# Feed-forward gated activations turned by VectorE block transposes instead of TensorE

## Reference

```python
D_FF = -(-8 * D_MODEL // (3 * 256)) * 256      # 5632

def swiglu(h, w_gate, w_up, w_down):
    return (jax.nn.silu(h @ w_gate) * (h @ w_up)) @ w_down

# in second_block, for each of 2 layers, after the mixer:
x = x + swiglu(rms_norm_2(x, norm_ffn[i]), ffn_w_gate[i], ffn_w_up[i], ffn_w_down[i])
```

## Time and profile before

| what | value |
|---|---|
| time, median of 3 runs | 3035.3 us |
| lowest and highest run | 3033.88 and 3035.71 us |
| span of the profiled execution | 3032.1 us (no other time of this execution is given) |
| TensorE busy | 3024.7 us |
| VectorE busy | 1712.5 us |
| ScalarE busy | 1546.5 us |
| GpSimd busy | 299.9 us |
| first FfnUp stage | about 1239 to 1728 us of the span |
| first FfnDown stage | about 1728 to 1965 us of the span |

### The profile page before, as it was taken

The page is one execution under the profiler, slowest core; times in us unless marked ns, Lnnn a source line. Parts: engine busy times, 40 slices in busy tenths (PEclk is TensorE's granted clock), DMA queues, the critical chain, the costliest instruction groups (busy, mean ns, idle before and its releaser), DMA issues.

```text
span 3032.1 us, 37463 instructions
## 1 busy us (share of the span) xinstructions
PE 3024.7 (100%) x14305; PEld 2532.1 (84%) x14305; DVE 1712.5 (56%) x2011; ACT 1546.5 (51%) x2125; POOL 299.9 (10%) x252
## 2 busy tenths in 40 slices
PE   9999999999999999999999999999999999999999
PEld 8888888988888888888888888888888888888887
DVE  5666655589555675544444455568855444444554
ACT  5556554555654664544444444467845444444443
POOL 1043200145000450000000000001000000000000
PEclk9999999999999999999999999999999999999999
DMA  9674335555445544555655555565455556555554
GB/s 312 199 234 154 129 128 180 164 184 175 139 157 190 181 152 140 185 190 181 197 189 180 195 193 193 190 201 178 140 200 188 183 185 199 184 183 196 192 192 151
DMA packets 256721, 551.84 MB, mean 182 GB/s; under 512 B 9728, under 2 KB 43264, under 8 KB 245856
## 3 DMA queue, kind: packets, MB, share of 16 engines
q1 hardware_dynamic: 255824, 548.79, 54.5%
q0 software_dynamic: 752, 1.48, 0.2%
q10 hardware_dynamic: 32, 0.01, 0.0%
HBM read 548.14 MB, written 2.10 MB: 181 GB/s over the span
## 4 chain that ended last, share of the span: by engine, by line
PE 98%; DVE 1%; ACT 0%; DMA 0%; issue 0%; SPq 0%
PE psum L734 42%; PE psum L2364 32%; PE psum L2502 16%; PE psum L2640 2%; PE psum L1462 2%; PE psum L1478 1%; PE psum L976 1%; PE psum L1490 1%; PE psum L2333 1%; PE psum L1451 1%; PE psum L2091 0%; DVE weights_lo L550 0%; PE psum L1686 0%; PE psum L1962 0%; PE psum L1465 0%; DMA proj<-in_mem 0%
## 5 line engine op out<-in xcount | busy, mean ns | idle before, releaser
L550 DVE TENSOR_TENSOR weights_lo<-weights,weights_hi 128x1024 fp32r<-128x1024 f32 (+2 forms) x1015 | 1259.1, 1251 | 1018.0 <-ACT weights_hi L532 1016.4
L532 ACT ACTIVATE weights_hi<-weights 128x1024 fp32r<-128x1024 f32 (+2 forms) x1015 | 1052.1, 1047 | 1200.2 <-PE psum L734 549.4
L734 PE MATMUL psum<-weights_hi,act_hi 128*128 128x512 f32 (+3 forms) x1952 | 764.3, 392 | 0.3 <-DVE weights_lo L550 0.2
L734 PE MATMUL psum<-weights_hi,act_lo 128*128 128x512 f32 (+3 forms) x1952 | 749.1, 384 | 0.0
L734 PE MATMUL psum<-weights_lo,act_hi 128*128 128x512 f32 (+3 forms) x1952 | 748.1, 383 | 0.0
L2364 PE MATMUL psum<-weights_hi,act_hi 128*128 128x512 f32 x1408 | 549.8, 391 | 0.0
L2364 PE MATMUL psum<-weights_hi,act_lo 128*128 128x512 f32 x1408 | 548.1, 389 | 0.0
L2364 PE MATMUL psum<-weights_lo,act_hi 128*128 128x512 f32 x1408 | 547.8, 389 | 0.0
L734 PEld LDWEIGHTS psum<-weights_hi,act_hi 128*128 128x128 f32 x1952 | 366.7, 188 | 69.1 <-issue 4.6
L734 PEld LDWEIGHTS psum<-weights_hi,act_lo 128*128 128x128 f32 x1952 | 366.3, 188 | 68.0
L734 PEld LDWEIGHTS psum<-weights_lo,act_hi 128*128 128x128 f32 x1952 | 367.2, 188 | 62.9
(11 more groups left out here) (262 smaller groups left out, 1921.3 us busy)
## 6 DMA issues: line engine op xcount, KB each, us to landing
weights<-in_ffn_w_gate SPq DMA_DIRECT2D x88, 1024.0 KB, 5.1
weights<-in_ffn_w_up SPq DMA_DIRECT2D x88, 1024.0 KB, 5.1
weights<-in_ffn_w_down SPq DMA_DIRECT2D x88, 1024.0 KB, 4.8
weights<-in_odd_w_in SPq DMA_DIRECT2D x40, 1024.0 KB, 5.1
weights<-in_even_w_in SPq DMA_DIRECT2D x36, 1024.0 KB, 5.0
weights<-in_w_out SPq DMA_DIRECT2D x32, 1024.0 KB, 5.0
weights<-in_rnn_w_in SPq DMA_DIRECT2D x32, 1024.0 KB, 5.3
weights<-in_attn_w_qkv SPq DMA_DIRECT2D x24, 1024.0 KB, 5.2
```

Source lines behind the costliest of these rows:

```text
L532: e.nc.scalar.activation(e.WH[(2 * slot + b) % HL][:, 0:n // 2], e.RAW[slot][:, b * n // 2:(b + 1) * n // 2], ACT.Copy).then_inc(self.hi.s ...
L550: e.nc.vector.tensor_tensor(e.WL[s][:, 0:n // 2], e.RAW[slot][:, b * n // 2:(b + 1) * n // 2], e.WH[s][:, 0:n // 2].bitcast(F32), ALU.subt ...
L734: last = e.nc.tensor.matmul(e.PS[:, banks.start + m, 0:w], a, x, start=(kk == 0 and n == 0), stop=(kk == KT - 1 and n == 2))
```

## The change

The turn of a chunk moves from TensorE to VectorE. A VectorE transpose turns 32x32 blocks; one instruction takes the 32 partitions (tokens) of block row `rows` of `HID`, and of every 128 channels the 32 of block column `cols`, for both row tiles and all four channel tiles: 2 x 4 x 32 = 256 elements a partition. It writes them turned to the 32 partitions of block column `cols` of `HT`. Sixteen such instructions turn one chunk, from SBUF to SBUF.

In FfnUp they are issued in pairs behind each of the eight low halves of granules 2 to 5 of the next chunk. For the last chunk they are issued in the first group of FfnDown: three behind each of the four low halves of granules 1 and 2, two behind each of the two of granule 3. The TensorE turn, ScalarE's copy and the waits on `hcopied` are gone. TensorE waits at the second half of the first down granule for the product alone (`hid`). ScalarE waits in groups 0 and 10 of FfnDown for the turned chunks. VectorE's FfnUp program is written out for all 11 chunks in place of a loop; TensorE's loop starts one chunk earlier.

```diff
@@ -275,6 +275,7 @@
         e.s_pv = Signal(ctx, nc, "s_pv")
         e.s_stored = Signal(ctx, nc, "s_stored")
         e.s_gate = Signal(ctx, nc, "s_gate")
+        e.s_blockturned = Signal(ctx, nc, "s_blockturned")
         e.s_hid = Signal(ctx, nc, "s_hid")
         e.s_hturned = Signal(ctx, nc, "s_hturned")
         e.s_hcopied = Signal(ctx, nc, "s_hcopied")
@@ -2221,14 +2222,16 @@
 
 class FfnUp(Stage):
 
+    BLOCKS = 16
+
     def __init__(self, e, prev, prep):
         gm = e.queue.pop(0)
         self.n = D_FF // CHUNK
         self.flip = e.parity
         self.views = gm["gate"]["view"], gm["up"]["view"]
         super().__init__(e, prev, 8 * self.n, prep)
-        self.gate, self.hid, self.hturned, self.hcopied = (s.mark() for s in (e.s_gate, e.s_hid, e.s_hturned, e.s_hcopied))
-        for s in (e.s_gate, e.s_hid, e.s_hturned, e.s_hcopied):
+        self.gate, self.hid, self.hturned = (s.mark() for s in (e.s_gate, e.s_hid, e.s_blockturned))
+        for s in (e.s_gate, e.s_hid, e.s_blockturned):
             s.advance(self.n)
         prep.end()
 
@@ -2248,16 +2251,6 @@
 
         return 2 * ((part + self.flip) % 2)
 
-    def copy_hidden(self, act, f):
-
-        e = self.e
-        act.wait_ge(self.hturned.sem, self.hturned.at(f + 1))
-        e.nc.scalar.activation(e.HT[:, bass.ds(f * 4, 4), :].rearrange("p k t -> p (k t)"),
-                               e.PS[:, 4:6, :].rearrange("p b n -> p (b n)"), ACT.Copy).then_inc(self.hcopied.sem, 1)
-
-    def carry_scalar(self, act):
-        self.copy_hidden(act, self.n - 1)
-
     def scalar(self, act):
         e = self.e
 
@@ -2269,8 +2262,6 @@
                     if q == 1:
                         self.prev.carry_scalar(act)
                     self.prep.after_hi(act, q)
-            if not first:
-                self.copy_hidden(act, f - 1)
             for q in range(4):
                 self.split_hi(act, f * 8 + 4 + q, q, f * 2 + 2)
                 if q == 0:
@@ -2292,55 +2283,53 @@
         e = self.e
         dve.wait_ge(self.used.sem, self.used.at(f * 16 + 16))
         dve.wait_ge(self.gate.sem, self.gate.at(f + 1))
-        if not isinstance(f, int) or f > 0:
+        if f > 0:
 
             dve.wait_ge(self.hturned.sem, self.hturned.at(f))
         for m in range(MT):
             ins = e.nc.vector.scalar_tensor_tensor(e.HID[:, m, :], e.PS[:, self.bank(1) + m, :], e.RS[:, m:m + 1], e.GATE[:, m, :], ALU.mult, ALU.mult)
         ins.then_inc(self.hid.sem, 1)
 
+    def turn(self, dve, f, first, count):
+
+        e = self.e
+        if first == 0:
+            dve.wait_ge(self.hid.sem, self.hid.at(f + 1))
+        for n in range(first, first + count):
+            rows, cols = divmod(n, 4)
+            src = e.HID[32 * rows:32 * rows + 32, :, :].rearrange("p m (k x c) -> p m k x c", k=4, x=4)[:, :, :, cols, :]
+            dst = e.HT[32 * cols:32 * cols + 32, 4 * f:4 * f + 4, :].rearrange("p k (m x t) -> p m k x t", m=MT, x=4)[:, :, :, rows, :]
+            ins = e.nc.vector.transpose(dst, src)
+        if first + count == self.BLOCKS:
+            ins.then_inc(self.hturned.sem, 1)
+
     def carry_vector(self, dve):
         self.product(dve, self.n - 1)
 
+    def carry_turn(self, dve, first, count):
+        self.turn(dve, self.n - 1, first, count)
+
     def vector(self, dve):
-        for q in range(4):
-            self.split_lo(dve, q, q)
-            if q == 1:
-                self.prev.carry_vector(dve)
-            self.prep.after_lo(dve, q)
-        for q in range(4):
-            self.split_lo(dve, 4 + q, q)
-
-        def body(f):
-            for q in range(4):
-                self.split_lo(dve, f * 8 + q, q)
-                if q == 1:
-                    self.product(dve, f - 1)
-            for q in range(4):
-                self.split_lo(dve, f * 8 + 4 + q, q)
-        body(1)
-        with dve.Fori(2, self.n) as f:
-            body(f)
-
-    def turn(self, pe, f, first):
-
-        e = self.e
-        pe.wait_ge(self.hid.sem, self.hid.at(f + 1))
-        if not first:
-            pe.wait_ge(self.hcopied.sem, self.hcopied.at(f))
-        for k in range(4):
-            for m in range(MT):
-                last = e.nc.tensor.transpose(e.PS[:, 4 + k // 2, (k % 2) * T + m * P:(k % 2) * T + (m + 1) * P],
-                                             e.HID[:, m, k * P:(k + 1) * P], e.CT[:, 0:P])
-        last.then_inc(self.hturned.sem, 1)
-
-    def carry_tensor(self, pe):
-        self.turn(pe, self.n - 1, False)
+        for f in range(self.n):
+            for g in range(8):
+                slot = 2 * (g - 2)
+                turning = f > 0 and 0 <= slot < self.BLOCKS // 2
+                between = (lambda dve, j: self.turn(dve, f - 1, 2 * slot, 2)) if turning else None
+                self.split_lo(dve, f * 8 + g, g % 4, between=between)
+                if turning:
+                    self.turn(dve, f - 1, 2 * slot + 2, 2)
+                if g == 1:
+                    if f == 0:
+                        self.prev.carry_vector(dve)
+                    else:
+                        self.product(dve, f - 1)
+                if f == 0 and g < 4:
+                    self.prep.after_lo(dve, g)
 
     def tensor(self, pe):
         e, prep = self.e, self.prep
 
-        def products(f, part, turn_at=None):
+        def products(f, part):
             first = isinstance(f, int) and f == 0
             for q in range(4):
                 if first and part == 0:
@@ -2366,14 +2355,10 @@
                     last.then_inc(self.used.sem, 1)
                 if first and part == 0:
                     prep.after_tensor(pe, q)
-                if q == 2 and turn_at is not None:
-                    self.turn(pe, *turn_at)
         products(0, 0)
         products(0, 1)
-        products(1, 0, (0, True))
-        products(1, 1)
-        with pe.Fori(2, self.n) as f:
-            products(f, 0, (f - 1, False))
+        with pe.Fori(1, self.n) as f:
+            products(f, 0)
             products(f, 1)
 
 
@@ -2440,15 +2425,18 @@
     def scalar(self, act):
         final = self.n - 1
 
+        up = self.prev
+
         def body(j):
+            if isinstance(j, int):
+
+                act.wait_ge(up.hturned.sem, up.hturned.at(up.n - 1 if j == 0 else up.n))
             for q in range(4):
                 if not (isinstance(j, int) and j == final and q == 3):
                     self.hidden_hi(act, j, q)
                 if isinstance(j, int) and j == final and q == 2:
                     self.hidden_hi(act, j, 3)
                 self.split_hi(act, j * 4 + q, q, j + 1)
-                if isinstance(j, int) and j == 0 and q == 1:
-                    self.prev.carry_scalar(act)
         body(0)
         with act.Fori(1, final) as j:
             body(j)
@@ -2464,9 +2452,13 @@
                     self.hidden_lo(dve, j, q)
                 if isinstance(j, int) and j == final and q == 2:
                     self.hidden_lo(dve, j, 3)
-                self.split_lo(dve, j * 4 + q, q)
-                if isinstance(j, int) and j == 0 and q == 0:
+                carry = isinstance(j, int) and j == 0
+                at = (None, (0, 3), (6, 3), (12, 2))[q]
+                self.split_lo(dve, j * 4 + q, q, between=(lambda dve, j: self.prev.carry_turn(dve, *at)) if carry and q else None)
+                if carry and q == 0:
                     self.prev.carry_vector(dve)
+                elif carry:
+                    self.prev.carry_turn(dve, at[0] + at[1], at[1])
         body(0)
         with dve.Fori(1, final) as j:
             body(j)
@@ -2516,9 +2508,7 @@
                         if first and h == 0 and m == 0:
                             pe.wait_ge(up.gate.sem, up.gate.at(up.n))
                         if first and h == 1 and m == 0:
-                            up.carry_tensor(pe)
-                        if first and h == 1 and m == 1:
-                            pe.wait_ge(up.hcopied.sem, up.hcopied.at(up.n))
+                            pe.wait_ge(up.hid.sem, up.hid.at(up.n))
                         last = self.products(None, h, m, hh, hl, q, (2 * q + h) % HL, 0, first)
                     last.then_inc(self.used.sem, 1)
                     if q == 1 and isinstance(j, int) and j == final:
```

## The result

The changed kernel takes 3014.54 us, median of 5 runs (3014.22 to 3019.92), against 3035.53 us before in the same comparison (5 runs, 3033.88 to 3040.33). The ratio of its runs to those of before is 0.9936, with a 95% interval of 0.9925 to 0.9947: 19.4 us less, between 16 and 23 (the two medians lie 21.0 apart). The profiled span is 3012.7 us. The prediction was 3015.9 us, with a span of 3012.7. It was right.

What follows compares the result with a forecast made beforehand. The prediction took TensorE's queue to bound the kernel. Removing the turns (19.1 us) and the wait for the copy (0.3), with added VectorE work costing 0, gave 19.4 off 3035.3: 3015.9 us, range 3012 to 3024.

Steps and rivals of the forecast that it cites:

- The turn: TensorE's transposes of each chunk leave its queue: 22 turns at 0.87 us, 19.1 us gained.
- The copy's wait: TensorE's idle time in two places until ScalarE's copy had emptied the banks goes away: 0.3 us gained.
- From span to time: Median of the runs stays 3.2 us above the profiled span, so span 3012.7 means time 3015.9 us.
- The transpose, t = 0.43: Start-to-start price of one VectorE block transpose, taken from subtraction L2438 on as many elements: 0.43 us.
- The covers: VectorE's idle time hides transposes up to 1.14 us each in the up stage, 0.68 in the down stage; cost 0.
- 16t - 18.3: Up stage: lateness of low half 12 in us per chunk with t us per transpose; positive only above 1.14.
- VectorE's new waits and the written-out program: VectorE's up stage: waiting for the previous chunk's turned signal, and writing out the loop, cost 0.
- the tightest point of the chunk: Up stage: conversions held behind ScalarE's blocked copy leave VectorE's subtractions least lead; this goes away, credited 0.
- R1: Down stage's first chunk: VectorE late at 0.68 to 1.14 us a transpose; 3029.3 us at 1.10; 5%.
- R2: Up stage: VectorE becomes the bound above 1.14 us a transpose; 3120 us at 1.397; 4%.
- R3: Chunk's matmuls: something other than TensorE's own queue sets their 43.54 us; no effect, time stays 3035.3; 2%.
- R4: Chunk edges: written-out VectorE stage and more semaphore traffic cost half the gain, 3025 us; 2%.

Runs made afterwards that it cites:

- experiment 2: Changed kernel with TensorE's 8 transposes put back beside VectorE's for ten chunks a layer, into banks nobody reads; span 3030.6 us, first up stage 488.5.
- 4: Changed kernel with every block transpose of the up stages issued twice, the copy into spare SBUF; span 3015.6 us, first up stage 479.6.
- 5: Changed kernel with the last chunk's block transposes, in the down stage's first group, issued twice; span 3017.3 us.
- experiment 6: Changed kernel with up-stage transposes tripled: span 3024.3 us with repeats to the same partitions in a row, 3099.0 when neighbours always write other partitions.
- 1: Changed kernel with one VectorE memset per chunk in place of its 16 block transposes; span 3014.2 us, first up stage 479.6.
- experiment 3: Kernel before with VectorE's up-stage program written out for all 11 chunks in place of its loop; span 3033.8 us, first up stage 488.5.
- experiment 8: Changed kernel with a chunk's 16 transposes in one run behind low half 9; median 3021.15 us, ratio 0.9953 to the kernel before.
- experiment 7: Changed kernel with a chunk's 16 transposes in one run right behind the product; median 3048.52 us, ratio 1.0043 to the kernel before.

## Why the prediction was right

**The bound.** TensorE's queue was the time, and it stayed so (experiment 2, and the chain after).

**The turn, 22 x 0.87 = 19.1 us.** Right and slightly short. In the earlier trace rows one turn stands 1344.24 - 1299.83 = 44.41 us behind the other, and 192 matmuls now take 43.52: a turn cost 0.89 in the first layer. In the second layer the up stage went from 2787.5 - 2298.6 = 488.9 us to 2769.0 - 2289.4 = 479.6 (starts of the same two groups there), so it cost 0.93. The chain's 0.87 leaves out what the matmuls next to the transposes lose. The two up stages gave 9.0 and 9.3 us, and the two down stages, each with a turn and a wait for the copy, some 0.9 each: the 20.1 of the path.

**The copy's wait, 0.3 us.** Too large, and a misreading of the earlier trace rows: the 0.3 us are the idle time of the weight load, not of TensorE's matmuls. The load and two matmuls of the kernel before, in the first down stage:

```profile
1732.35 0.19 PEld L2502 LDWEIGHTS psum<-weights_hi,act_hi 128*128 128x128 f32 x1 [0.17 <-ACT ffn_hidden_t L2255]
```

```profile
1732.22 0.39 PE L2502 MATMUL psum<-weights_hi,act_lo 128*128 128x512 f32 x1
1732.45 0.40 PE L2502 MATMUL psum<-weights_hi,act_hi 128*128 128x512 f32 x1
```

The matmul of that load started 0.23 us after the one before it, nearly as always. What the wait cost can be no more than some hundredths of a microsecond a layer. So the sum of 19.4 met the measured 19.4 by three small errors that cancel: the turns gave more, the copy's wait next to nothing, and what precedes the stage took 0.7 more.

**From span to time.** The prediction added 3.2 us to the span, a median of several runs less the span of one. In the profiled execution of the changed kernel the time is 3014.32 us and the span 3012.7, 1.6 apart. The forecast of the time, 3015.9, came within 1.4 us of the median all the same.

**The transpose, t = 0.43.** Measured 0.436 us of duration and 0.45 from start to start. The low half before it also lost its overlap in seven gaps of eight: 1.26 us to the next start in place of the 1.16 assumed. Both were under the cover, so the sum did not move. The row that gave the price, L2438 at 425 ns for as many elements, was a good one, and so was not crediting its overlap.

**The covers, 1.14 us in the up stage and 0.68 in the down stage.** That the one is wide and the other thin shows in the experiments: 0.77 a slot does nothing in the first and stalls the second (4 and 5); 1.10 is just past the edge of the first, 1.34 far past it (6). The first limit lies between 0.77 and 1.10, so 1.14 was a little too high. The stalls themselves were 0.43 and 4.33 us a chunk where 16t - 18.3 gives none and 3.1. The term leaves out the 0.1 us by which seven of eight low halves before a transpose grow (0.7 in all) and the 0.23 us by which a weight load wants its half before the matmul.

**VectorE's new waits and the written-out program, 0.** Right (experiments 1 and 3). The product's new wait is for a signal raised eight low halves earlier (behind low half 11, where the product stands behind low half 3), not some 15; nothing hangs on it.

**ScalarE.** The copies' 22.6 us went, but its busy time fell by 17.6, not 22.6. In the earlier trace rows the copy fills only 0.92 us up to the next start, and the two conversions behind it take 2.00 together, where each alone takes 1.06: 22 x (0.92 - 0.12) = 17.6. The prediction also said that the tightest point of the chunk goes away with the copy, and this was wrong. It had only looked at the copy; the wait for the gate product leaves 1.9 us at low half 10, before and after, and experiment 8 ran into it.

**The rivals.** R1 did not occur: VectorE's first down group is full for 19.7 us, where the prediction had some 10, and the nearest, low half 6, was 2.4 us early. R2, the bound moving to VectorE, is what experiment 6 made at t = 1.34, and experiment 7 made by placement alone. R3 is refuted by experiment 2. R4's written-out stage is refuted by experiment 3, and its cost at chunk edges does not show: the chunks follow each other at 43.52 us, 192 steps of 0.2267.

## What to carry to other kernels

When one engine's queue is the whole time, work moved off it is gained at its start-to-start price on that queue, even if it costs eight times as much on an engine with idle time: here 0.9 us of TensorE against 7.2 us of VectorE a chunk. What the idle engine can take is not set by its busy share but by how late each single hand-over may be: list for every step when it is ready and when it is wanted, and spread the added work so that no step uses up its own lead. The same sixteen instructions made the kernel 19 us faster in pairs and 13 us slower in one run.

## What the runs showed of the hardware

- VectorE block transposes of 32x256 fp32 take 436 ns, and 0.45 us from start to start if each writes another group of 32 partitions than the one before. If they read and write the same groups again, three take 1.10 us instead of 1.34. A 128x1024 subtraction of 1.23 us is followed after 1.15 us by a transpose that reads and writes the first group, and after 1.26 by one that reads or writes another.
- The 8 TensorE transposes of 128x128 fp32 among matmuls cost 0.89 us of TensorE's time in the first layer and 0.93 in the second, though one lasts 272 ns by itself.
- A late weight half is wanted by its weight load, some 0.23 us before the matmul's own start. In three kernels the load started 0.28, 0.49 and 1.71 us late and 0.20, 0.43 and 1.61 us a chunk were lost. A half that was ready for its matmul's own turn, within a hundredth of a microsecond, still cost the 0.20.
